# VectorE's weight splits before ScalarE's results, bound to the raw buffer two chunks on

## The reference

```
proj = rms_norm(x) @ w_in
x = x + (sum over three mixers of sigmoid(gate) * (y @ w_p)) @ w_o
x = x + (silu(h @ w1) * (h @ w3)) @ w2
```

## Time and profile before

| what | value |
|---|---|
| median of three runs | 3302.48 us |
| the profiled execution's own time | 3303.02 us |
| its span, first to last instruction | 3301.2 us |
| TensorE busy | 3250.4 us, 98% |
| VectorE busy | 1788.3 us, 54% |
| ScalarE busy | 1306.4 us, 40% |
| GpSimd busy | 590.0 us, 18% |
| granted TensorE clock, mean | 0.997 |

### The profile page before, as it was taken

The page is one execution under the profiler, slowest core; times in us unless marked ns, Lnnn a source line. Parts: engine busy times, 40 slices in busy tenths (PEclk is TensorE's granted clock), DMA queues, the critical chain, the costliest instruction groups (busy, mean ns, idle before and its releaser), DMA issues.

```text
span 3301.2 us, 38212 instructions
## 1 busy us (share of the span) xinstructions
PE 3250.4 (98%) x15436; PEld 2698.1 (82%) x15436; DVE 1788.3 (54%) x2716; ACT 1306.4 (40%) x1989; POOL 590.0 (18%) x492
## 2 busy tenths in 40 slices
PE   8999999999999999999999999999999999999998
PEld 7887788888887888788888888888888888788887
DVE  6864565444438654655444455553644268974433
ACT  5643453332226533633322333332432238843221
POOL 1420132011003210330110011120211023531101
PEclk9999999999999999999999999999999999999999
DMA  3122323223221122223222322222223323223322
GB/s 135 33 72 72 105 88 102 96 96 102 91 97 58 59 71 78 99 87 101 95 97 90 112 80 86 80 83 96 94 92 102 96 83 96 96 77 102 102 96 83
DMA packets 84994, 295.60 MB, mean 90 GB/s; under 512 B 9425, under 2 KB 11985, under 8 KB 84817
## 3 DMA queue, kind: packets, MB, share of 16 engines
q1 hardware_dynamic: 84816, 293.15, 27.4%
HBM read 291.02 MB, written 2.10 MB: 89 GB/s over the span
## 4 chain that ended last, share of the span: by engine, by line
PE 85%; DVE 7%; ACT 3%; POOL 2%; issue 2%; DMA 1%; SPq 0%; POOLq 0%; DVEq 0%; ACTq 0%
PE bank L312 83%; PE bank L315 2%; DVE wl L559 1%; POOL u_g L579 1%; DMA raw<-in_wts 1%; DVE small L1263 1%; ACT wh L532 1%; DVE m_ptl L559 1%; DVE u_uc L555 0%; ACT c_k L532 0%; DVE m_qf L549 0%; DVE u_t L555 0%; ACT m_p L535 0%; DVE b_qk L549 0%; DVE b_p L566 0%
## 5 line engine op out<-in xcount | busy, mean ns | idle before, releaser
L559 DVE TENSOR_TENSOR wl<-raw,wh 128x1024 fp32r<-128x1024 f32 (+1 forms) x531 | 663.5, 1252 | 785.3 <-ACT wh L532 783.4
L312 PE MATMUL bank<-zh,wh 128*128 128x512 f32 (+1 forms) x2652 | 1029.4, 388 | 13.8 <-ACT zh L532 7.6
L312 PE MATMUL bank<-zh,wl 128*128 128x512 f32 (+1 forms) x2652 | 1021.0, 385 | 2.2 <-DVE wl L559 2.2
L312 PE MATMUL bank<-zl,wh 128*128 128x512 f32 (+1 forms) x2652 | 1020.1, 385 | 3.0 <-DVE zl L562 2.9
L532 ACT ACTIVATE wh<-raw 128x1024 fp32r<-128x1024 f32 (+1 forms) x531 | 555.7, 1051 | 538.9 <-PE bank L312 484.0
L312 PEld LDWEIGHTS bank<-zh,wh 128*128 128x128 f32 x2652 | 500.6, 189 | 114.4 <-ACT zh L532 7.6
L312 PEld LDWEIGHTS bank<-zh,wl 128*128 128x128 f32 x2652 | 500.4, 189 | 106.1 <-DVE wl L559 5.8
L312 PEld LDWEIGHTS bank<-zl,wh 128*128 128x128 f32 x2652 | 500.8, 189 | 98.7 <-DVE zl L562 3.9
L312 PE MATMUL bank<-f_mh,wh 128*128 128x512 f32 (+1 forms) x748 | 284.7, 381 | 0.0
L312 PE MATMUL bank<-f_mh,wl 128*128 128x512 f32 (+1 forms) x748 | 282.8, 378 | 1.2 <-DVE wl L559 1.2
L312 PE MATMUL bank<-f_ml,wh 128*128 128x512 f32 (+1 forms) x748 | 281.7, 377 | 0.0
(11 more groups left out here) (337 smaller groups left out, 4437.0 us busy)
## 6 DMA issues: line engine op xcount, KB each, us to landing
raw<-in_wts SPq DMA_DIRECT2D x529, 512.0 KB, 3.3
c_nb<-in_c_bias SPq DMA_DIRECT2D x16, 384.0 KB, 3.1
x<-in_xT SPq DMA_DIRECT2D x8, 256.0 KB, 6.3
out<-x SPq DMA_DIRECT2D x16, 128.0 KB, 1.8
b_mask<-in_b_mask SPq DMA_DIRECT2D x2, 576.0 KB, 4.4
r_d<-in_decay SPq DMA_DIRECT2D x4, 256.0 KB, 2.7
raw<-in_wts SPq DMA_DIRECT2D x2, 256.0 KB, 3.4
m_t<-in_mla_tab SPq DMA_DIRECT2D x2, 256.0 KB, 4.9
```

What stands on the lines that cost most here:

```text
L312: return self.e.matmul(out, l, r, start=start, stop=stop, skip_group_check=inside)
L559: return self.e.tensor_tensor(out, src, b32(hi), ALU.subtract)
```

## The change

`Dve` gets its own `weights`, which lowers the second of the two bounds by the number of raw buffers:

```diff
 class Dve(Splitter):
+    def weights(self, upto, least=-1):
+
+        super().weights(upto, least - RAWS)
+
     def tt(self, out, a, b, op):
         return self.e.tensor_tensor(out, a, b, op)
```

## The result

The changed kernel takes 3327.14 us (median of 4 runs, 3326.26 to 3328.57), the kernel before 3302.87 in the same comparison: a ratio of 1.0077, with a 95% interval of 1.0065 to 1.0089, so it is slower; between the two medians lie 24.3 us, 0.7%. A second comparison, of five runs of the changed kernel on one chip, gave 3325.13 against 3301.81 (1.0074, 1.0061 to 1.0087), 23.3 us. The profiled execution has a span of 3326.8 us.

The account below looks back on a forecast made before the run. TensorE, busy 98% of the span, bounds the kernel. Terms of 15.3 us in both layers' mixers, 2.3 in retention and -0.3 in post-norms sum to 17.3 on 3303.0, so about 3320 us; range 3310 to 3330, down to 3306 with rival 2.

Parts of the forecast that it names:

- Chunk 14: Latent attention: the split moves behind the reciprocal and `m_ptl`, `m_qf` comes later, TensorE pays 0.94 us.
- chunk 15: Latent attention: a moved split delays the scaling of `m_p` in the same way, 1.0 us.
- chunk 13: Latent attention: `m_ptl` comes earlier, but the unit behind it is held by the later minimum; 0.2 us.
- chunks 16 to 18: Latent attention: the first has an earlier `m_ptl` but a later minimum, the second costs 0.3 us, the third has cover.
- Chunks 21, 22 and 23: First dilated half: the split shuts out GpSimd's scaling of `b_p`; TensorE pays 0.9, 0.33 and 0.68 us.
- Chunks 35 and 36: Second dilated half: TensorE waits longer for `wl`, 0.67 us more, then a new stall of 0.85 us.
- Chunk 297: Retention: two `r_ql` go ahead of the split TensorE waits for; 2.3 us later, 1.2 at least.
- Chunk 59: Neighbourhood attention: the split lands under GpSimd's addition and scalings; 0.6 us, between 0 and 1.
- chunks 24 and 25: First dilated half: the split delays GpSimd's `b_p`; 0.67 us with 0.2 of slack, then 0.5 us.
- paid in full: Whole kernel: TensorE is busy 98% of the span, so every new stall costs its length unless a later one swallows it.
- Post-norms: `zl` would be ready some 1.6 us earlier, most handed on; gain 0.3 us, bounds -2.5 and 0.
- Rival 1: Whole kernel faster: ScalarE's results served 1.2 us earlier, stalls on `zl` and `m_ptl` go, 6.4 us, 3296; chance 0.13.

Follow-up runs that it names:

- the experiment that keeps the two apart: The changed kernel with one more wait: in the first dilated half VectorE holds its let-stand splits until GpSimd has scaled the probabilities; 3316.34 us.
- the six parts: The kernel before, bound loosened for one stage at a time: 3308.26 (dilated, first half), 3308.14 (latent), 3305.47 (retention), 3299.13 (post-norms), 3303.60 (dilated, second half), 3302.86 us (neighbourhood).
- the first dil half: The kernel before, bound loosened only for chunks 21 to 26 and 167 to 172, the dilated attention's first half in both layers; 3308.26 us.
- that with mla: The kernel before, bound loosened for latent attention and the dilated attention's first half together (chunks 11 to 18, 21 to 26, 157 to 164, 167 to 172); 3314.40 us.
- the doubled scaling: The kernel before, no split moved; GpSimd first scales the first unit's probabilities by 1.0 in the first dilated half, once per layer; 3306.42 us.

## Why the prediction was right, and where it was not

**Sign and size.** About 3320 was predicted, 3327.1 measured, inside the range of 3306 to 3330. The forecast, not a rival, came true, and the main mechanism (the split shuts out GpSimd's scaling, TensorE waits for it) is shown by the experiment that keeps the two apart. Every row named as its sign is there (`b_p` on GpSimd 0.91 to 1.81, TensorE's wait for it 2.2 to 10.3 where 8 was said, `wl` +5.0 for +5, chunk 36 a new wait, the wait for `zl` short, scalings of `m_p` above 1.5 us down from ten to two, and mla's minimums at chunks 14 and 15 up to 0.94 us later against the matmuls around them).

The size is 7 us above the sum. Some 3 of these are terms set too low, some 3 to 4 the clock, which no term had. The range held all the same, but 3310 does not follow from the bounds of the terms: added up as they stand they give -0.5 to +25.7 us, 3302 to 3328, so the result is near the top of them.

**Term by term**, from the jumps in the first profile, layer 0. Chunk 14: 0.74 for 0.94; chunk 15: 0.80 for 1.0; chunk 13: 0.14 for 0.2; the places of chunks 16 to 18: -0.36, +0.60 and +0.32 for 0.3. Chunks 21, 22 and 23: 0.94, 0.35 and 0.70 for 0.9, 0.33 and 0.68. Chunks 35 and 36: 0.66 and 0.87 for 0.67 and 0.85. Chunk 297: 2.28 for 2.3. Chunk 59: 0.80 for 0.6, and nbr has 0.3 a layer more near chunk 49, which was to have slack; that makes +2.3 for +1.2.

**Term mis-sized: chunks 24 and 25**, 1.22 and 1.03 for 0.67 and 0.5. The step "it would end 0.78 behind" the split was right for a split that stands alone. Here another VectorE instruction on two operands follows within the time in which GpSimd is held up, and GpSimd stays shut out through that one too: the split ends at 223.13, `b_qk` at 223.72, the scaling at 224.42, 0.70 later. That is 2 us over both layers (in layer 1 chunk 24 gives 1.03), some two thirds of what the waits alone are above the sum (20.6 for 17.3). The Trainium skill (SBUF — State Buffer, "SBUF: two separate sides") has it that the engine that starts first gets the shared ports for its whole instruction. The trace agrees for the split but for 0.13 us (the scaling of 0.91 us ends 0.78 behind it), and shows beside it that the waiting engine did not get its turn between two VectorE instructions.

**Term left out: the clock.** The prediction has every new wait "paid in full" and no more. In fact a wait of about 2 us can be followed by matmuls at 1.2 GHz. It costs 1.6 us behind chunk 297 in one profile of the changed kernel and some 2.5 in the other, and 1.5 to 3.4 us behind chunk 21. The kernel before paid this too, at 1098, 1358 and 2921. The net is what is left between the 20.6 us of waits and the measured 24.3 and 23.3: some 3 to 4 us, as the mean clock of the runs has it (3.7).

**Post-norms.** "0.3 is left" was too little, for both reasons: the waits alone gain 1.0, and the slow stretch behind the old wait of 2.15 us goes with it, so that the profiles have -3.1 and -3.3, past the term's bound of -2.5. That most of the gain is handed on was right (0.7 of 1.66 at once, and nothing left of it at 2313.9). Rival 1 named this place rightly, and was wrong about the kernel: the waits for `m_ptl` did go (2.7 to 0.4 us), but later waits took up what they gave.

**What stays open.** I can't say which of two equal waits will be followed by the lower clock. The wait for `b_p` of 1.9 us at chunk 21 stands in ten places of five profiles (the changed kernel twice, the first dil half, that with mla, the doubled scaling); in four of them the clock fell. Behind chunk 297's wait of 3.8 us it fell in all four profiles that have it, behind the `zl` wait of 2.15 us in seven of eight, behind `f_g`'s 2.57 us in 18 of 26 places. Nor is a single long wait needed, as the windows at 154.90 and 2919.40 show. And the six parts' measured sum of 16.5 is below the traces' 20.6; their intervals are too wide to say whether that is chance. By their means and the mean clock the parts have 18.3 us of waits and 0.9 of clock, the whole 20.7 and 3.7, so if something is missing it is the clock more than the waits.

## What to carry to other kernels

An idle time put down to a release ("idle before, ended by `wh`") is worth something only if what stands behind it in the queue could have run; here 785 us of it stood ahead of the splits, and loosening their places took 5 away and cost 24. Before an instruction is moved into a "free" slot, look at what the neighbouring engine is issued in that slot: a split of 1.2 us right behind the reciprocal that starts GpSimd's scaling costs TensorE 0.9 us, and holding it back until the scaling is done costs nothing. On a kernel at 98% TensorE, look at its single waits of 2 us and more first, since a stretch at half clock can follow them: moving the one split ahead of such a wait gained 3 us, moving 61 cost 24.

## What the runs showed of the hardware that I had not expected

- The granted TensorE clock fell from 2.4 to 1.2 GHz in the middle of a busy stream behind a single wait of 1.9 us, and came back after 3 to 7 us, while matmuls ran without a break (1147.20 to 1154.40: 0.56 on average). It did so in one run and not in the next of the same kernel, at the same matmul (chunk 21 of layer 0: 0.51 in 187.00:190.00, 1.00 in 188.90:192.00).
- A GpSimd scaling of 0.91 us took 2.32 when a VectorE instruction of 1.21 us and one of 0.68 ran back to back over it.
